# Second feed-forward entered by halves of the tokens: the last output-projection tile in two halves and two banks, three tiles over sixteen half k-steps

## The reference, cut to what matters

```python
x = x + g1 * (mixed @ w_out[l])

h = rms_norm_2(x, norm2_g[l]) * (1 + sc2) + sh2
u = causal_depthwise_conv(h @ w_up[l], conv_w[l], conv_b[l])
u_gate, u_val = jnp.split(u, 2, axis=-1)
x = x + g2 * ((jax.nn.silu(u_gate) * u_val) @ w_down[l])
```

## Time and profile before

| | us |
|---|---|
| median of 3 runs | 1424.2 (1423.99 to 1424.27) |
| the profiled execution, its own time | 1424.42 |
| its span in the profile | 1422.5 |
| PE busy | 1379.6 (97%) |
| DVE busy | 887.1 (62%) |
| ACT busy | 590.1 (41%) |
| POOL busy | 70.3 (5%) |
| mean granted clock of PE | 0.99 |

### The profile page before, as it was taken

The page is one execution under the profiler, slowest core; times in us unless marked ns, Lnnn a source line. Parts: engine busy times, 40 slices in busy tenths (PEclk is TensorE's granted clock), DMA queues, the critical chain, the costliest instruction groups (busy, mean ns, idle before and its releaser), DMA issues.

```text
span 1422.5 us, 18346 instructions
## 1 busy us (share of the span) xinstructions
PE 1379.6 (97%) x6316; PEld 1092.1 (77%) x6316; DVE 887.1 (62%) x1454; ACT 590.1 (41%) x967; POOL 70.3 (5%) x128
## 2 busy tenths in 40 slices
PE   7999999999989999999998999999989999999999
PEld 5777777767868888888884788767668888888887
DVE  5666667777676777774336777866556565655222
ACT  5445544453353323233223633666454444344111
POOL 4000000000001212120000000000000000000000
PEclk9999999999999999999998999999999999999999
DMA  5222222213215556555431211121112323233332
GB/s 187 103 74 67 68 74 74 74 60 104 100 60 163 191 193 198 193 186 167 137 125 46 88 60 60 60 74 60 58 58 89 103 88 103 88 103 115 93 96 85
DMA packets 42321, 146.74 MB, mean 103 GB/s; under 512 B 5392, under 2 KB 5664, under 8 KB 42272
## 3 DMA queue, kind: packets, MB, share of 16 engines
q1 hardware_dynamic: 34448, 120.39, 25.9%
q0 software_dynamic: 7824, 25.70, 5.4%
HBM read 143.97 MB, written 2.10 MB: 103 GB/s over the span
## 4 chain that ended last, share of the span: by engine, by line
PE 91%; DVE 5%; ACT 2%; issue 1%; DMA 0%; SPq 0%; DVEq 0%; ACTq 0%
PE bank L601 64%; PE bank L714 12%; PE bank L671 3%; PE bank L736 2%; PE bank L939 2%; PE bank L755 2%; PE bank L773 1%; PE bank L641 1%; PE bank L628 1%; DVE hbuf L1635 0%; DVE w_lo L1586 0%; DVE gate_last L1776 0%; DVE gate_a L1776 0%; PE bank L776 0%; ACT w_hi L1104 0%
## 5 line engine op out<-in xcount | busy, mean ns | idle before, releaser
L1586 DVE TENSOR_TENSOR w_lo<-raw,w_hi 128x1024 fp32r<-128x1024 f32 (+2 forms) x225 | 271.7, 1210 | 165.6 <-ACT w_hi L1104 160.2
L1104 ACT ACTIVATE w_hi<-raw 128x1024 fp32r<-128x1024 f32 (+2 forms) x225 | 233.1, 1037 | 300.9 <-PE bank L601 278.1
L601 PE MATMUL bank<-h_hi,w_hi 128*128 128x512 f32 x872 | 345.0, 396 | 0.5 <-DVE w_lo L1586 0.5
L601 PE MATMUL bank<-h_hi,w_lo 128*128 128x512 f32 x872 | 339.7, 390 | 0.0
L601 PE MATMUL bank<-h_lo,w_hi 128*128 128x512 f32 x872 | 339.6, 389 | 0.0
L601 PEld LDWEIGHTS bank<-h_hi,w_hi 128*128 128x128 f32 x872 | 163.7, 188 | 41.9 <-issue 8.1
L601 PEld LDWEIGHTS bank<-h_hi,w_lo 128*128 128x128 f32 x872 | 163.7, 188 | 34.5
L601 PEld LDWEIGHTS bank<-h_lo,w_hi 128*128 128x128 f32 x872 | 163.8, 188 | 33.7 <-issue 1.0
L601 PE MATMUL bank<-f_hi,w_lo 128*128 128x512 f32 x352 | 136.9, 389 | 0.0
L601 PE MATMUL bank<-f_hi,w_hi 128*128 128x512 f32 x352 | 136.9, 389 | 0.0
L601 PE MATMUL bank<-f_lo,w_hi 128*128 128x512 f32 x352 | 136.9, 389 | 0.0
(11 more groups left out here) (305 smaller groups left out, 1856.5 us busy)
## 6 DMA issues: line engine op xcount, KB each, us to landing
raw<-in_w_up SPq DMA_DIRECT2D x66, 512.0 KB, 3.3
raw<-in_w_mix SPq DMA_DIRECT2D x48, 512.0 KB, 3.3
ada<-in_w_ada POOLq DMA_DIRECT2D x96, 256.0 KB, 3.2
raw<-in_w_down SPq DMA_DIRECT2D x32, 512.0 KB, 3.5
raw<-in_w_in SPq DMA_DIRECT2D x25, 512.0 KB, 3.3
raw<-in_w_gate SPq DMA_DIRECT2D x22, 512.0 KB, 3.3
raw<-in_w_out SPq DMA_DIRECT2D x16, 512.0 KB, 3.4
raw<-in_w_down SPq DMA_DIRECT2D x16, 384.0 KB, 3.7
```

The lines of the kernel that those rows point to most:

```text
L601: last = pe.matmul(to[:, :], wt[:, slot, k, :], act_[:, rhs0 + k, :], start=(k == first and n == 0), stop=(k == K - 1 and n == 2))
L1104: act.activation(w_hi[:, s, k0:K, :], raw[:, s, k0:K, :], ACT.Copy).then_inc(hi_ready[s], 1)
L1586: dve.tensor_tensor(w_lo[:, s, k0:K, :], raw[:, s, k0:K, :], w_hi[:, s, k0:K, :].bitcast(F32), ALU.subtract).then_inc(split_ready[s], 1)
```

## The change

The last tile (t = 7) is computed for tokens 0 to 255 into bank O1 and then for tokens 256 to 511 into bank S1, 24 products of 256 columns each. The sums of squares go to S0 for the first half and to O0 for the second. Between the first half and the rest PE issues the two sums over `sqacc`, and the sum over the first half's last squares comes after three k-steps of the second half. ACT and DVE square, normalize, modulate and split half by half (16 steps instead of 8). The second half's last x, squares and inverse root, and the split of the slot 1 tile, are put between steps of the first half. On PE three tiles (T0, T1, G1) take the halves as they come, in 16 half k-steps, the third with a lag of 7. In round 0 of the convolution the split of slot 0 is moved ahead of the taps on both engines.

```diff
--- before.py
+++ after.py
@@ -390,6 +390,10 @@
         gy_f32, gy_hi, gy_ready = signal("gy_f32"), signal("gy_hi"), signal("gy_ready", credit=1)
         stored = signal("stored", 16)
 
+        half_out, half_sq, half_x = signal("half_out"), signal("half_sq"), signal("half_x")
+        TOKENS = (slice(0, S // 2), slice(S // 2, S))
+        SUMS = (S0, O0)
+
         def col(name, k=0):
 
             return cols[:, bass.ds(k + VEC_AT[name], 1)]
@@ -611,6 +615,57 @@
                 last = products(to, slot, hi, lo, k0, k1, **kw)
                 if k1 == KU:
                     last.then_inc(unit_done[slot], 1)
+
+            def sum_of_half(h, sums=SUMS):
+
+                signal_ = sq_g[1] if h else half_sq
+                pe.wait_ge(signal_, w.next(signal_, times=4 if h else 1))
+                pe.matmul(sums[h][:, TOKENS[h]], ones[:, :], sq[:, 1, TOKENS[h]], start=False, stop=True).then_inc(ms_ready, 1)
+
+            def last_tile_by_halves(to, parts, hi, lo, sums=SUMS):
+
+                steps = [(slot, k, rhs0 + k, k == K - 1) for slot, K, rhs0 in parts for k in range(K)]
+                for h, t in enumerate(TOKENS):
+                    for n, (slot, k, rhs, ends) in enumerate(steps):
+                        if h and n == 3:
+                            sum_of_half(0, sums)
+                        if h == 0 and k == 0:
+                            pe.wait_ge(split_ready[slot], w.next(split_ready[slot]))
+                        for m, (wt, act_) in enumerate(((w_hi, hi), (w_hi, lo), (w_lo, hi))):
+                            last = pe.matmul(to[h][:, t], wt[:, slot, k, :], act_[:, rhs, t], start=(n == 0 and m == 0),
+                                             stop=(n == len(steps) - 1 and m == 2))
+                        if h and ends:
+                            last.then_inc(unit_done[slot], 1)
+                    if h == 0:
+                        last.then_inc(half_out, 1)
+                        w.skip(sq_g[0], 4)
+                        w.skip(sq_used[1], 4)
+                        pe.wait_ge(sq_used[0], w.next(sq_used[0], times=4))
+                        for half, of in enumerate(TOKENS):
+                            pe.matmul(sums[half][:, of], ones[:, :], sqacc[:, of], start=True, stop=False)
+
+            def three_units_by_halves(to, slots, lag, between={}):
+
+                for slot in slots[0:2]:
+                    pe.wait_ge(split_ready[slot], w.next(split_ready[slot]))
+                for n in range(2 * KU + lag):
+                    if n == lag:
+                        pe.wait_ge(split_ready[slots[2]], w.next(split_ready[slots[2]]))
+                    if n < 2 * KU:
+                        pe.wait_ge(h_ready, w.next(h_ready))
+                    for g, slot in enumerate(slots):
+                        i = n - lag if g == 2 else n
+                        if not 0 <= i < 2 * KU:
+                            continue
+                        h, k = divmod(i, KU)
+                        t = TOKENS[h]
+                        for m, (wt, act_) in enumerate(((w_hi, h_hi), (w_hi, h_lo), (w_lo, h_hi))):
+                            last = pe.matmul(to[g][:, t], wt[:, slot, k, :], act_[:, k, t],
+                                             start=(k == 0 and m == 0), stop=(k == KU - 1 and m == 2))
+                        if i == 2 * KU - 1:
+                            last.then_inc(unit_done[slot], 1)
+                    if n in between:
+                        between[n]()
 
             def sum_squares():
 
@@ -865,10 +920,11 @@
                     pe.wait_ge(read0, w.next(read0, ahead=1))
                     unit(G0, 0, h_hi, h_lo)
 
-                two_units((T0, T1), (0, 2))
                 if not squares:
-                    up()
+                    pe.wait_ge(read1, w.next(read1, ahead=1))
+                    three_units_by_halves((T0, T1, G1), (0, 2, 1), 7, {1: lambda: sum_of_half(1)})
                 else:
+                    two_units((T0, T1), (0, 2))
                     unit(S1, 1, h_hi, h_lo)
                     pe.wait_ge(x_sum, 1)
                     pe.matmul(S0[:, :], ones[:, :], sqacc[:, :], start=True, stop=True).then_inc(ms_ready, 1)
@@ -1075,10 +1131,12 @@
                 else:
                     if t >= 5:
                         pe.wait_ge(drained_x[(t - 5) % 2], (t - 5) // 2 + 2)
-                    unit(w_out_bank(t), t % SLOTS, y_hi, y_lo)
+                    if t < KD - 1:
+                        unit(w_out_bank(t), t % SLOTS, y_hi, y_lo)
+                    else:
+                        last_tile_by_halves((w_out_bank(t), S1), [(t % SLOTS, KU, 0)], y_hi, y_lo)
             for g in range(2):
                 w.skip(drained_x[g], 4, ahead=1)
-            sum_squares()
             ffn(conv_gd, conv_vd, False)
             down(drained_x)
 
@@ -1114,6 +1172,26 @@
                     act.sem_inc(sq_used[1], 1)
                 then(act.activation(rstd[:, :], sums[:, :], ACT.Ln, scale=1.0 / D, bias=eps6[:, :]))
                 act.activation(rstd[:, :], rstd[:, :], ACT.Exp, scale=-0.5).then_inc(rstd_ready, 1)
+
+            def inverse_rms_of_half(h, sums=SUMS, buffered=True):
+
+                t = TOKENS[h]
+                act.wait_ge(ms_ready, w.next(ms_ready))
+                if h and buffered:
+                    act.sem_inc(sq_used[1], 1)
+                then(act.activation(rstd[:, t], sums[h][:, t], ACT.Ln, scale=1.0 / D, bias=eps6[:, :]))
+                act.activation(rstd[:, t], rstd[:, t], ACT.Exp, scale=-0.5).then_inc(rstd_ready, 1)
+
+            def modulated_hi_by_halves(gain, shift, between):
+
+                for i in range(2 * KD):
+                    h, k = divmod(i, KD)
+                    t = TOKENS[h]
+                    act.wait_ge(xr_ready, w.next(xr_ready))
+                    then(act.activation(hbuf[:, k % 2, t], hbuf[:, k % 2, t], ACT.Identity, scale=gain(k), bias=shift(k)))
+                    act.activation(h_hi[:, k, t], hbuf[:, k % 2, t], ACT.Copy).then_inc(n_hi, 1)
+                    if i in between:
+                        between[i]()
 
             def modulated_hi(gain, shift):
 
@@ -1521,11 +1599,23 @@
             for t in range(KD - 1):
                 split_hi(t % SLOTS, by_halves=(t == 0))
                 x_tile(t % 2, t)
-            x_tile(1, 7)
-            w.start(unit_done, "ffn_2")
-            inverse_rms()
-            split_hi(1)
-            modulated_hi(lambda k: mod_a[:, 1, k:k + 1], lambda k: modc[:, 24 + k:25 + k])
+            act.wait_ge(sq_used[1], w.next(sq_used[1], ahead=1))
+            act.wait_ge(half_x, w.next(half_x))
+            act.activation(sq[:, 1, TOKENS[0]], xT[:, 7, TOKENS[0]], ACT.Square).then_inc(half_sq, 1)
+            inverse_rms_of_half(0)
+
+            def square_of_second_half():
+
+                act.wait_ge(drained_x[1], w.next(drained_x[1]))
+                act.activation(sq[:, 1, TOKENS[1]], xT[:, 7, TOKENS[1]], ACT.Square).then_inc(sq_g[1], 1)
+
+            def third_tile_hi():
+
+                w.start(unit_done, "ffn_2")
+                split_hi(1)
+
+            modulated_hi_by_halves(lambda k: mod_a[:, 1, k:k + 1], lambda k: modc[:, 24 + k:25 + k],
+                                   {1: square_of_second_half, 2: third_tile_hi, 4: lambda: inverse_rms_of_half(1)})
 
             def conv_tap(t, bank_, to, ready):
 
@@ -1535,13 +1625,16 @@
             act.preload_act_table_set("silu_and_others")
             def conv_round(j, gate, up, done, free):
 
+                if done == 2:
+                    split_hi(0)
                 act.wait_ge(unit_done[done], w.next(unit_done[done]))
                 conv_tap(j + NF, up, cval, conv_v)
                 if done == 1:
                     split_hi(1)
                 act.wait_ge(unit_done[0], w.next(unit_done[0]))
                 conv_tap(j, gate, cgate, conv_g)
-                split_hi(0)
+                if done == 1:
+                    split_hi(0)
                 act.wait_ge(free, w.next(free))
                 act.activation(sil[:, :], cgate[:, :], ACT.Silu).then_inc(silu_r, 1)
                 act.wait_ge(f_f32, w.next(f_f32))
@@ -1617,6 +1710,29 @@
                     if k >= 1:
                         lo(k - 1)
                 lo(KD - 1)
+
+            def modulated_lo_by_halves(between):
+
+                def lo(i):
+                    h, k = divmod(i, KD)
+                    t = TOKENS[h]
+                    dve.wait_ge(n_hi, w.next(n_hi))
+                    dve.tensor_tensor(h_lo[:, k, t], hbuf[:, k % 2, t], h_hi[:, k, t].bitcast(F32),
+                                      ALU.subtract).then_inc(h_ready, 1)
+
+                for i in range(2 * KD):
+                    h, k = divmod(i, KD)
+                    if h and k == 0:
+                        lo(i - 1)
+                    if k == 0:
+                        dve.wait_ge(rstd_ready, w.next(rstd_ready))
+                    dve.wait_ge(h_ready, w.next(h_ready, ahead=2))
```

(29 more changed lines are left out.)

## The result

The changed kernel takes 1429.55 us (median of 6, 1426.08 to 1430.52) against 1424.16 for the kernel before (6, 1423.74 to 1425.24): slower by 5.4 us. Its profiled execution took 1429.28 us with a span of 1426.9.

What follows compares the result with a forecast made beforehand. PE, busy 97%, bounds the kernel, so time is won only where it waits. The second `up` 3.3 us later plus 0.5 for the clock makes 3.8 us slower, median 1424.2 to 1428.0; range 1424.6 to 1430.8.

Steps and rivals of the forecast that it cites:

- the supply of the half-steps: ACT and DVE making feed-forward k-tiles: 16 half-steps need 16 us where 8 whole ones needed 11.8, spending the early start.
- the wait that takes the place of the one removed: PE before the second `up`: a new wait of 2.5 us for slot 1's split, `up` starting 3.3 us later.
- step 3: Feed-forward half-step supplied by ACT and DVE: held up by `split_lo(1)` on DVE, ready only at 1059.0.
- step 15: Last of the sixteen feed-forward half-steps from ACT and DVE: ready at 1072.8, after one each 1.0 us.
- I take 0.5 of these together: Clock falls behind the new hole before `up` (0 to 1.7 us) or while PE is starved (at most 0.6): 0.5 us.
- 2.0 us were lost behind the hole: Kernel before, first feed-forward products after the norm: 48 took 12.85 us at the lower clock, would need 10.9.
- the ceiling: Most the change could win, from PE's hole at the norm and the lower clock behind it: some 8.5 us, less the sums.
- halves in proportion to their width: Rival: each ACT, DVE and PE operation takes half the time, +0.2 us, 1424.4; chance 0.22 with its neighbours within 0.2%.
- the third tile late alone: Rival: round 0's chain is 2.5 us shorter or overlapped, so just +0.75 us stays, 1425.0; chance 0.06.
- dearer half products: Rival: a half product on PE costs 0.14 to 0.16 us, +4.6 to +6.6, 1429 to 1431; chance 0.08.
- unhidden weight loads: Rival: a half product on PE costs as much as a whole, 0.227 us: +15 us, 1439; chance 0.03.
- the reordering of round 0: `split_hi(0)` ahead of the taps: spares PE 2.5 us at `gate`, but next `up` starts no sooner: net nothing.

Runs made afterwards that it cites:

- e3: Changed kernel with ten unused 512-column products between the first `gate` and the second `up`, where PE waited: 1427.44 us, 1.0024 to the kernel before.
- e5: Kernel before with 19 unused 512-column products in the hole between the norm's last sum and the first feed-forward product: 1422.90 us, ratio 0.9992.
- e4: Changed kernel with last tile, sums of squares and inverse root whole as before; sixteen half-steps, three tiles and new round 0 order kept: 1428.98 us, 1.0036.
- e6: Changed kernel with cheaper half-steps: gain in DVE's multiplication, shift in its subtraction, one ACT operation instead of two: 1424.80 us, 1.0008 to the kernel before.
- e1: Changed kernel with the split of slot 0 put back behind the taps of round 0 on ACT and DVE: 1427.42 us, 1.0028 to the kernel before.
- e2: Changed kernel with the third tile in S1 instead of G1 and slot 1's split moved into round 0 behind its taps: 1425.50 us, ratio 1.0008.
- e8: Kernel before with the cheaper steps at whole width and 17 unused products in the hole before the feed-forward: 1421.41 us, ratio 0.9981.
- e7: e2 with e6's cheaper half-steps and a lag of 4 instead of 7 for the third tile: 1422.26 us, 0.9986 to the kernel before.

## Why the prediction was right, and where it was off

The prediction was right, and for its reasons: the sign, the supply of the half-steps and the wait that takes the place of the one removed were as stated. By steps, with 0.39 taken off the prediction's times: half products 0.120 apart, measured 0.12; last tile's end 1052.5, measured 1052.4; first feed-forward product 1054.16, measured 1053.86; step 3 ready 1058.6, measured 1058.4; step 15 at 1072.4, measured 1072.2; third tile's end 1076.9, measured 1076.55; `split_lo(1)` done 1084.66, measured 1084.45; second `up` 1084.9, measured 1084.50. Against the kernel before that is +3.0 where I had +3.3. (The 12.85 us of the earlier trace rows run to the end of the last product, so my 1076.5 and 1082.0 for the kernel before are some 0.1 late.) Half-wide operations measured 0.42, 0.42, 0.48 and 0.59 us, as computed from whole ones.

The mis-sized term is the clock's: "I take 0.5 of these together". Filling the hole (e3) won 2.1 us, and 10 of 12 executions are in the slower group of times. The nearest row, a hole of 3.07 us between starts with a fall behind it, was the better guide than the middle between it and zero; 3.0 + 2.1 is 5.1 of the 5.4 measured. The measured time lies in the range, just above the forecast's own range of 1427.1 to 1429.5.

Two readings on the kernel before were off without weight for the sum. "2.0 us were lost behind the hole" to the clock: with the clock up (e5) only 1.0 us of B comes back, since the supply holds PE next. And the ceiling, 7.5 + 2.0, is 9.5 us less the sums and not 8.5; by e5 it is smaller still.

Of the rivals, halves in proportion to their width is refuted by the 0.42 rows; the third tile late alone by the wait of 2.3 us; dearer half products and unhidden weight loads by the distance of 0.12. Each of these products has a full-array load of 0.19 us, so the loads run beside products. That is against the rule which the prediction took from the Trainium skill (TensorE: Matmul & The Clock Gate, The mechanism of packing), that a load overlaps a running product only in another row group; the same section also lets a load be pulled ahead into a background weight buffer, and with that sentence the trace agrees. The fixed part of short instructions, which the Trainium skill names in its rule on 512 elements (VectorE: DVE Perf Modes, the section on the TRN2 errata), shows in DVE's 0.42 us for 256 columns where 512 take 0.69; e4's third tile, 2.2 us late, is at least in part its price, and e6, with an instruction less in each step, takes 2.7 us away.

That the reordering of round 0 is worth nothing by itself was right for the start of the `up` and wrong for the time: with the old order (e1) the `up` starts as late, and the median is 2.1 us lower by the clock. The part in which the wait lost 2.4 us and the supply the rest was right as well (e2 and e6 each take out one of them).

## What to carry to other kernels

Before work is cut into halves to start a consumer sooner, count the supply of the pieces: here the start came 4.0 us sooner, and the sixteen shorter steps (2.9 us, with one weight split between them) and the rest of the work put between them (1.7 us) took all of it. Then follow the chain behind the stage to the next weight slot and bank that the consumer wants again, since less consumer work now lies over it. If the consumer is at a lower clock behind its hole, fewer operations in each supply step and any harmless work in the hole can be worth as much as the earlier start (e8 is 0.85 us below e7, and needs no halves).

## What the runs showed of the hardware

A wait of PE of 2.3 us was followed by about 3.4 us at the lower clock in both profiles of the changed kernel, and by none in e1's, where it lay 5.4 us earlier, in e6's, 2.7 us earlier, and in e4's. By the grouping of the times (10 of 12 above 1428, against 2 of 7 in e1 and 3 of 11 above 1426 in e6) it is so in most executions of the one kernel and in few of the others; the mean clock of the executions goes with that grouping (0.990 to 0.992 in the slow groups, 0.992 to 0.995 in the fast ones). With ten products of no use in the wait the clock stayed up in e3's profile, and with 17 or 19 in the longer hole of the kernel before it did in e8's and e5's. A stretch in which PE was busy 3.33 of 5.0 us kept the upper clock in the changed kernel's profile, and the same stretch was followed by 0.50 in e2's. Full-array products of 256 columns with a weight load each run 0.12 us apart, though a load alone is recorded with 0.19 us.
